# Depthwise convolution of a Conformer block: three of eight channel chunks moved from tap-by-tap accumulation to block Toeplitz products on TensorE over four token phases

## What is computed

```python
CONV_WIDTH = 31
def conv_module(x, w_pw1, b_pw1, w_dw, b_dw, ln_g, ln_b, w_pw2, b_pw2):
    h = x @ w_pw1 + b_pw1
    h = h[..., :D_MODEL] * jax.nn.sigmoid(h[..., D_MODEL:])
    h = lax.conv_general_dilated(
        h, w_dw[:, None, :], window_strides=(1,), padding=[(CONV_HALF, CONV_HALF)],
        dimension_numbers=('NWC', 'WIO', 'NWC'), feature_group_count=D_MODEL) + b_dw
    h = jax.nn.silu(layer_norm(h, ln_g, ln_b))
    return h @ w_pw2 + b_pw2
```

## Time and profile before

| | us |
|---|---|
| median of three runs | 2747.21 (2746.41 to 2748.06) |
| the profiled execution, first to last instruction | 2743.8 |
| convolution stage in it: from the first `up` of the second halves to the last `taps` | 563.0 to 746.0 |
| wait from there until `stats(0)` starts on PE | 4.6 |

### The profile page before, as it was taken

One profiled execution on the slowest core, in us unless ns is written; L12 is line 12 of the kernel. 1 busy time (PEld: TensorE's weight loads), 2 busy tenths in 40 slices (PEclk: granted clock), 3 DMA queues, 4 the chain that ended last, 5 costly groups with the idle time before them and its releaser, 6 DMA issues.

```text
span 2743.8 us, 36352 instructions
## 1 busy us (share of the span) xinstructions
PE 2665.3 (97%) x14266; PEld 2460.2 (90%) x14266; DVE 1423.0 (52%) x2553; ACT 986.2 (36%) x1647; POOL 1613.6 (59%) x874
## 2 busy tenths in 40 slices
PE   7999999999899999999999999999899999999998
PEld 7899999888678899999898999998899788999998
DVE  5643333669967643333664433337766476433335
ACT  4232332446543232332432322334445242323323
POOL 2576776669733576776636866674211234768665
PEclk9999999999999999999999999999999999999999
DMA  3222221311012222221421212232000111212213
GB/s 136 74 68 71 83 77 47 138 62 47 31 39 77 85 70 70 85 76 48 161 85 62 77 54 70 77 128 77 9 24 30 71 77 69 78 62 77 80 59 123
DMA packets 55464, 201.45 MB, mean 73 GB/s; under 512 B 6144, under 2 KB 6656, under 8 KB 55296
## 3 DMA queue, kind: packets, MB, share of 16 engines
q1 hardware_dynamic: 49248, 177.12, 19.5%
q10 hardware_dynamic: 6048, 22.02, 2.1%
HBM read 186.53 MB, written 12.58 MB: 73 GB/s over the span
## 4 chain that ended last, share of the span: by engine, by line
PE 80%; DVE 11%; POOL 5%; issue 3%; ACT 2%; DMA 0%; SPq 0%; POOLq 0%; DVEq 0%; ACTq 0%
PE ps L958 26%; PE ps L959 26%; PE ps L960 26%; POOL pacc L945 4%; DVE raw_sum L1625 2%; POOL w_lo L905 1%; DVE sum L1625 1%; DVE x L1643 1%; PE ps L1058 1%; DVE y L1632 1%; DVE y L1649 1%; PE ps L1194 1%; DVE pair L1523 0%; DVE xn L1696 0%; ACT w_hi L1252 0%
## 5 line engine op out<-in xcount | busy, mean ns | idle before, releaser
L905 POOL TENSOR_TENSOR w_lo<-w_stage,w_hi 128x1024 fp32r<-128x1024 f32 (+1 forms) x455 | 1019.3, 2268 | 576.1 <-ACT w_hi L1252 570.1
L958 PE MATMUL ps<-xn,w_hi 128*128 128x384 f32 x1920 | 646.9, 337 | 5.7 <-issue 4.2
L959 PE MATMUL ps<-xn,w_hi 128*128 128x384 f32 x1920 | 643.3, 335 | 0.0
L960 PE MATMUL ps<-xn,w_lo 128*128 128x384 f32 x1920 | 642.9, 335 | 0.0
L1252 ACT ACTIVATE w_hi<-w_stage 128x1024 fp32r<-128x1024 f32 (+1 forms) x455 | 436.5, 983 | 79.2 <-POOL w_stage L916 55.0
L958 PE MATMUL ps<-w_hi,hid 128*128 128x512 f32 x1056 | 412.7, 391 | 4.9 <-DVE y L1637 3.4
L960 PE MATMUL ps<-w_hi,hid 128*128 128x512 f32 x1056 | 411.4, 390 | 0.0
L959 PE MATMUL ps<-w_lo,hid 128*128 128x512 f32 x1056 | 411.3, 390 | 0.0
L958 PEld LDWEIGHTS ps<-xn,w_hi 128*128 128x128 f32 x1920 | 361.5, 188 | 9.5 <-issue 7.8
L959 PEld LDWEIGHTS ps<-xn,w_hi 128*128 128x128 f32 x1920 | 361.6, 188 | 1.7
L960 PEld LDWEIGHTS ps<-xn,w_lo 128*128 128x128 f32 x1920 | 361.3, 188 | 0.0
(11 more groups left out here) (196 smaller groups left out, 4034.1 us busy)
## 6 DMA issues: line engine op xcount, KB each, us to landing
w_stage<-weights SPq DMA_DIRECT2D x311, 512.0 KB, 3.6
x_kept<-x ACTq DMA_DIRECT2D x18, 512.0 KB, 2.6
x<-x_kept ACTq DMA_DIRECT2D x18, 512.0 KB, 7.0
g_pre<-rows SPq DMA_DIRECT2D x7, 512.0 KB, 5.3
x<-x_in SPq DMA_DIRECT2D x6, 512.0 KB, 7.9
g_post<-rows SPq DMA_DIRECT2D x6, 512.0 KB, 5.5
x<-x_in ACTq DMA_DIRECT2D x6, 512.0 KB, 8.0
y_out<-x SPq DMA_DIRECT2D x5, 512.0 KB, 2.6
```

The lines of the kernel that those rows point to most:

```text
L905: pool.tensor_tensor(w_lo[:, s, 0:n], w_stage[:, s, 0:n], w_hi[:, s, 0:n].bitcast(F32), ALU.subtract).then_inc(w_split, 1)
L958: pe.matmul(out, a[0], m[0], start=start, stop=False)
L959: pe.matmul(out, a[0], m[1], start=False, stop=False)
L960: return pe.matmul(out, a[1], m[0], start=False, stop=stop)
```

## The change

Chunks 0 to 4 lose their share on PE: all 31 taps go to DVE (20) and to ACT with POOL (11 products, 10 additions). Chunks 5 to 7 leave DVE, ACT and POOL altogether. For them `glu` writes the chunk in phase order (token 4n + i at phase i, place n); sixteen small DMAs a chunk on SP (`send`) regroup 32 channels x 4 phases onto the 128 partitions; for each of four groups of 32 channels DVE multiplies a 128x32 diagonal pattern with a table of tap values into nine 128x128 block Toeplitz matrices (`spread`, 1152 columns), PE makes nine products of 196 columns (`taps`), DVE takes the sums out with the bias (`gather`), and sixteen more small DMAs a chunk (`bring`, the last four on ACT's queue) carry them to `co`. `tap_w` and its building on ACT are gone. Input rows are put in phase order outside the kernel, and output rows back, so the order of tokens differs through the whole kernel; the work on them is the same outside the convolution. `stats` reads `co` with other addresses, 54 transposes in place of 48. The table `spread_in` is loaded before the stage's first weights, after a wait on the last pair product of the FFN ahead of it, and the rows `g_post` and `g_pre` are loaded at the end of the stage, since their places now hold the regrouped chunks.

```diff
-PE_TAPS = (0, 4, 4, 4, 5, 6, 8, 11)
-POOL_TAPS = (9, 9, 9, 9, 8, 8, 8, 10)
-DVE_TAPS = [TAPS - p - g for p, g in zip(PE_TAPS, POOL_TAPS)]
+CHAINS = 5
+POOL_TAPS = (11,) * CHAINS
+DVE_TAPS = [TAPS - g for g in POOL_TAPS]
...
+PHASES = 4
+GROUP = P // PHASES
+STEPS = 9
+SPREAD = STEPS * PHASES
...
         def taps(c):
-            s.add(1.34 * PE_TAPS[c], "taps", c)
-            tapped[c] = s.clock if c < KT - 1 else 0.0
-            splits()
...
+            for r in range(PHASES):
+                g = PHASES * (c - CHAINS) + r
+                s.add(3.05, "taps", c, r, g)
+                pool_until(s.clock)
+                dve_until(s.clock)
+                if g + 2 < GROUPS:
+                    on_dve(1.3, "spread", g + 2)
+                if r % 2 == 1:
+                    on_dve(0.6, "gather", c, r // 2)
+                splits()
...
         for c in range(2, KT):
             item(c, 0)
-            taps(c - 1)
-            if c > 2:
-                s.add(0, "tap_w", c)
+            if c == CHAINS + 1:
+                for g in range(2):
+                    on_dve(1.3, "spread", g)
+                taps(CHAINS)
             item(c, 1)
-        taps(KT - 1)
+        for c in range(CHAINS + 1, KT):
+            taps(c)
+        s.add(0, "bring_last")
...
+            def send(c):
+                to = phased[(c - CHAINS) % 2]
+                ...
+                sp.wait_ge(up_done, work.q[1, c, 1] + 1)
+                for r in range(PHASES):
+                    for j in range(PHASES):
+                        sp.dma_start(to[quarter(j), r, :], phases(c)[quarter(r), j, :]).then_inc(sent[c - CHAINS], 16)
+            def bring(c):
+                for a in range(2):
+                    sp.wait_ge(gathered, 2 * (c - CHAINS) + a + 1)
+                    for r in (2 * a, 2 * a + 1):
+                        ...
+                        for q in range(PHASES):
+                            sp.dma_start(out_place(c, r, q), sums_out(c)[quarter(q), r, :]).then_inc(brought[c - CHAINS], 16)
...
+                if u == UNIT0[1]:
+                    sp.wait_ge(pair_done, 4 * (CHUNKS - PLAIN) // 2)
+                    sp.dma_start(spread_v[:, :], spread_in).then_inc(spread_loaded, 16)
...
+                if u == row_unit(1, 3):
+                    send(CHAINS)
+                    bring(CHAINS)
+                elif u == row_unit(1, 5):
+                    send(CHAINS + 1)
+                elif u == row_unit(1, 7):
+                    send(CHAINS + 2)
+                    bring(CHAINS + 1)
+                    bring(CHAINS + 2)
+                    row(g_pre[:, :], PW2_ROW, pre_loaded)
+                    row(g_post[:, :], POST_ROW + 1, post_loaded)
...
+            def taps(c, r, g):
+                if r == 0:
+                    pe.wait_ge(sent[c - CHAINS], 16 * PHASES * PHASES)
+                if g >= PHASES and r % 2 == 0:
+                    pe.wait_ge(gathered, g // 2 - 1)
+                pe.wait_ge(spread_done, g + 1)
+                for m in range(STEPS):
+                    mm = pe.matmul(ps[:, 6 + r // 2, r % 2 * 2 * P:r % 2 * 2 * P + OUT_N],
+                                   spread_w[:, g % 2, m * P:(m + 1) * P],
+                                   phased[(c - CHAINS) % 2][:, r, m:m + OUT_N], start=m == 0, stop=m == STEPS - 1)
...
+            def spread(g):
+                if g >= 2:
+                    dve.wait_ge(taps_full, g - 1)
+                diagonal = spread_v[:, GROUPS * SPREAD:GROUPS * SPREAD + GROUP]
+                dve.tensor_tensor(spread_w[:, g % 2, :].rearrange("p (s n) -> p s n", s=SPREAD),
+                ...
+                                  ALU.mult).then_inc(spread_done, 1)
```

More of the change, by code:

```diff
@@ L374, in dve_until @@
             nonlocal dve
-            while dve < clock and at_d[0] < inputs[0] and at_d[0] in tapped:
+            while dve < clock and at_d[0] < inputs[0]:
                 c, j = at_d
-                if j == 0:
-                    dve = max(dve, tapped[c])
                 if j < DVE_TAPS[c]:
@@ L399, in item @@
             dve_until(s.clock + 0.7)
-            s.add(0, "glu", b, c, half, s.q[b, c, half])
-            dve += 0.7
+            while half == 0 and at_d[0] < c + 1 - CIN_SLOTS:
+                dve_until(dve + 1)
+            on_dve(0.9, "glu", b, c, half, s.q[b, c, half])
             if half == 1:
-                inputs[0] = c + 1
+                inputs[0] = min(c + 1, CHAINS)
             splits()
         def taps(c):
-            s.add(1.34 * PE_TAPS[c], "taps", c)
-            tapped[c] = s.clock if c < KT - 1 else 0.0
-            splits()
-        s.add(0, "tap_w", 1)
+            for r in range(PHASES):
[8 more added lines that the diff above has]
+                splits()
         item(0, 1)
-        s.add(0, "tap_w", 2)
         item(1, 1)
@@ L582, in plan, with trunk @@
     return s
-def trunk(nc, x_in, weights, vectors, rows, rope_in, ident_in, y_out, x_kept):
+def trunk(nc, x_in, weights, vectors, rows, rope_in, spread_in, ident_in, y_out, x_kept):
     work = plan()
@@ new lines, in glu, with gated @@
+                gated(c, q, ((near, 0, PHASES, NEAR), (far[:, 0:1, :], PROMPT, 1, P)) if half == 0
+                      else ((far[:, 1:, :], 0, PHASES - 1, P),))
+            def gated(c, q, parts):
+                for to, f, i, n in parts:
+                    a, gate = (t[:, f:f + i * n].rearrange("p (i n) -> p i n", i=i)
+                               for t in (ps[:, 2 * (q % 2), :], act_out[:, q % 2, :]))
+                    ins = dve.scalar_tensor_tensor(to, a, v("b_pw1", c), gate, ALU.add, ALU.mult)
+                ins.then_inc(up_done, 1)
@@ new lines, in glu_phased @@
+            def glu_phased(c, half, q):
+                if half == 0:
+                    dve.wait_ge(conv_done, c + 1 - CIN_SLOTS)
+                    for n in (0, FAR, IN_N - PHASES):
+                        dve.memset(phases(c)[:, :, n:n + PHASES], 0.0).then_inc(pads, 1)
+                near = phases(c)[:, :, PHASES:PHASES + NEAR]
+                far = phases(c)[:, :, FAR + PHASES:FAR + PHASES + P]
+                gated(c, q, ((near, 0, PHASES, NEAR), (far[:, 0:1, :], PROMPT, 1, P)) if half == 0
+                      else ((far[:, 1:, :], 0, PHASES - 1, P),))
@@ L1905, in _ @@
                     convolved(*at)
+                elif kind == "spread":
+                    spread(*at)
+                elif kind == "gather":
+                    gather(*at)
                 elif kind == "stats":
@@ L2007 @@
     column("w_dw", a["l0_conv_w_dw"].reshape(TAPS, KT, P).transpose(1, 0, 2))
+    w_dw, b_dw = a["l0_conv_w_dw"], a["l0_conv_b_dw"]
+    by_tap = np.zeros((PHASES, GROUP, GROUPS, SPREAD), np.float32)
+    bias = np.zeros((PHASES, GROUP, GROUPS), np.float32)
+    for g in range(GROUPS):
+        c0 = CHAINS * P + g * GROUP
+        for j in range(PHASES):
+            for n in range(SPREAD):
+                if 0 <= n + j - PHASES < TAPS:
+                    by_tap[j, :, g, n] = w_dw[n + j - PHASES, c0:c0 + GROUP]
+            bias[j, :, g] = b_dw[c0:c0 + GROUP]
+    diagonal = np.concatenate([np.eye(GROUP, dtype=np.float32)] * PHASES)
+    spread = np.concatenate([by_tap.reshape(P, -1), diagonal, bias.reshape(P, -1)], 1)
     rows = np.zeros((ROWS, D_MODEL), np.float32)
```

181 lines of the change are left out of this document (113 added, 68 removed).

## The result

The changed kernel took 2754.07 us (median of 12 runs, 2749.12 to 2758.02) against 2748.27 for the kernel before on the same chip (12 runs): 1.0019 times as long, with a 95% interval of 1.0011 to 1.0026. The forecast was 2746.6 and "no measurable change". The time lies inside the range (2734 to 2758), but what was measured is a loss of 3 to 7 us where a gain of 0.6 was forecast.

The account below looks back on a forecast made before the run. DVE's list with its late sigmoids was taken as the bound. From 2747.2 us, -2.5 in the stage, +0.65 at stats(0) and +1.2 at the stage's start gave 2746.6, range 2734 to 2758.

Parts of the forecast that it names:

- DVE as the bound, with its ledger: Convolution stage: DVE's work of 146.7 us plus 24.3 of waits puts the last sums out at 744.7; gain 2.5 us.
- The six waits: DVE's waits in the stage, for late sigmoids, a POOL addition and PE's use of the first matrices: together 24.3 us.
- PE's 20 us turned into waits: PE in the stage: 20.2 us less work, but it all becomes waits, about 13 us of them ahead of taps(5).
- Spread: Twelve spreads on DVE: 1.40 us each, 16.8 in all, plus 6.0 for the six that run beside POOL.
- Rival C: Spread and POOL shut each other out; a spread beside POOL takes 3.5 us: +10, 2756.6 us; chance 0.15.
- glu with a stride: glu on DVE, output stride of four elements: no extra time taken, at most 0.3 us each, 4 in all.
- An issue of a small DMA: SP's small DMAs for regrouping chunks: issues 0.47 us apart, the last landing 2.0 us later.
- rival D: An issue of the small DMAs takes 1 us rather than 0.47; taps(5) starts 8 us later: 2761 us; chance 0.07.
- stats(0) and behind: End of the stage: stats(0) starts 2.5 us earlier, then its three extra transposes cost 0.65 us.
- The start of the stage: Ahead of the stage: first weights land later, at about 509, making DVE's addition late: +1.2 us, bounds 0 and 5.

Follow-up runs that it names:

- e1: The changed kernel again, no edit, for a second profile: 2751.03 us, ratio 1.0011 to the kernel before.
- f1: e2 with the planner booking 2.25 us (even chunks) and 1.95 (odd) per POOL addition instead of 1.85: 2739.53 us, ratio 0.9961 to before.
- f2: e2 with 2.5 and 1.95 us booked per POOL addition, POOL's taps shared unevenly over chunks, each glu planned 1.7 us earlier: 2738.36 us, ratio 0.9959.
- f3: e2 with spread writing only 128 of 1152 columns from the third group on (output wrong, same matmuls): 2749.43 us, ratio 0.9999 to before.
- f4: e2 with PE doing up(6,1) ahead of taps(5) instead of behind it: 2752.45 us, ratio 1.0015 to before.
- e2: The changed kernel with SP's wait for the feed-forward pair and the table load eight weight units later: 2747.26 us, ratio 0.9999 to before.
- e3: The kernel before plus only SP's wait for the last feed-forward pair ahead of the stage's first weights: 2754.23 us, ratio 1.0021 to before.
- h1: f2 with ACT issuing rows 2 and 3 of send(7) and rows 0 and 2 of bring(7), SP the rest: 2738.79 us, ratio 0.9963.
- e4: The kernel before again, no edit, for a second profile: one run of 2746.08 us.
- g1: The kernel before with 2.25 us (even chunks) and 1.95 (odd) booked per POOL addition instead of 1.9: 2748.08 us, ratio 0.9996 to before.
- g2: f2 with ACT issuing rows 2 and 3 of send(7) and rows 0, 1 and 3 of bring(7), SP the rest: 2738.04 us, ratio 0.9964.
- g3: f2 once more, no further edit, for a second profile and more runs: 2738.43 us, ratio 0.9961 to the kernel before.

## Why the prediction was wrong

By its own steps:

- **DVE as the bound, with its ledger: right.** Forecast 174.4 us from `glu(1,1)` to the end of the last `convolved`; measured 755.30 - 580.63 = 174.7, and 174.8 in e1. The six waits were forecast at 10.0, 3.3, 1.2, 4.0, 3.4 and 2.4 (24.3) and came at 9.7, 2.9, 1.0, 2.9, 3.1 and 3.5 (23.2). f1 to f4 show that the mechanism is the one named. That the sum fits to 0.3 us is part luck: in that stretch DVE was busy for 147.1 us and not busy for 27.6, where 150.1 and 24.3 had been counted.
- **PE's 20 us turned into waits: right.** 13.4 us ahead of `taps(5)` (13 forecast). A group took 12.21 / 4 = 3.05 at the full clock (2.9 forecast from 0.160 a record; it is 0.170), the first four 14.1 with waits and half the clock (13.3).
- **Spread: right in sum.** The last six took 9.3 us, four of them 1.36 or less and two 1.9 and 2.0; the first six 14.6, that is 6.5 more than six times 1.35, against the 6.0 allowed. By the rule quoted from the Trainium skill, "SBUF — State Buffer", "Who interferes with whom", the trace agrees (1.36 alone, 2.62 to 2.88 at 682 to 694, where POOL is busy throughout). Rival C used the same rule, and its 10 us did not come.
- **glu with a stride: at its upper bound.** 0.93 us for 384 columns in chunks 0 to 4, where the output has a stride of four elements, 0.62 in chunks 5 to 7 and before. I took none and kept 0.3 each as a bound; it is 0.3, some 2 us over the seven in the ledger.
- **An issue of a small DMA: 0.63 us, not 0.47.** The sixteen of `send(5)` were issued from 674.6 to 684.1 and landed by 686.0. By the difference it moved `taps(5)` by 2.4 us, and f4 gives no sign that this cost anything; rival D, at 1 us an issue, did not come.
- **stats(0) and behind: right.** Up to `stats(0)` the stage gained 1.9 to 2.0 us against before (2.5 forecast), and up to `down` it gave back 0.9 to 1.2 (0.65 forecast).
- **The start of the stage: the step that failed.** Forecast +1.2, with bounds 0 and 5; measured 3.1 and 3.7 in the two profiles up to `glu(1,1)`, 3.3 to 3.8 in time by e2, and 5.8 to 7.4 by e3 in the kernel before. I followed the chain to the first row only: weights at 509, a split on ACT, two on POOL, the gain at 517.2, the addition. That part was nearly right (in e1 the weights landed at 509.5, the gain ended at 517.9 and the addition was 2.1 late). What I put at nothing is what POOL's late work does to DVE beside it: the next two splits stretched the addition by 0.9, and the gain of the second row, late by 5.2, held a small DVE instruction for 2.1. The wait for that gain is not the reason: by my own durations it would have ended at 522.0 + 2.4 = 524.4, and before, DVE used it only at 523.4, so it would have added nothing to the 1.2. I had priced this contention for `spread` (rival C), where it cost nothing in time, and not here, where DVE had no slack.
- **Not foreseen at all:** 4.7 to 4.8 us near 1975, in the three profiles of the changed kernel (the first, e1 and e2).

Sum, with e1: -1.9 + 0.9 + 3.1 + 4.8 = +6.9 in the profile (7.1 read, beside 0.3 of earlier shift), and +4.2 in time in e1, +5.8 in the first measurement. Without the failed step (e2) the change is within 0.1% of before in time, which is what its other terms said. How much of the loss near 1975 is in those times is not known.

## What to carry to other kernels

When a change puts a wait ahead of a load, follow the load through every engine that consumes it, and past the first thing that becomes late: here DVE waited 2.1 us for the first late row, and lost another 3.0 because POOL's late work now ran beside DVE instructions that it holds up. When work is taken from one of several engines that were matched, the planner's numbers have to be fitted again before the change is judged: one number (1.85 to 2.25 and 1.95) was worth 10 us after the change, 5 of them seen in the queues, and nothing that could be measured before it. A long wait on the engine that was relieved can be a symptom of who feeds it: here moving its work (f4) only changed which engine was named as the cause.

## What was not expected of the hardware

**The clock near 1975.** The two longest idle times of PE are the same in both kernels there. Timeline rows of PE's transposes of the attention, in the changed kernel and then in before, and the granted clock in stretches (columns as above) of the changed kernel and of before:

```profile
1952.49 0.73 PE L1240 MATMUL ps<-ident,act_out 128*128 128x128 f32 x4 [2.12 <-DVE act_out L1960]
...
1971.40 0.66 PE L1240 MATMUL ps<-ident,act_out 128*128 128x128 f32 x4 [2.96 <-DVE act_out L1960]
```
```profile
1946.29 0.66 PE L1139 MATMUL ps<-ident,act_out 128*128 128x128 f32 x4 [2.12 <-DVE act_out L1822]
...
1965.21 0.66 PE L1139 MATMUL ps<-ident,act_out 128*128 128x128 f32 x4 [2.97 <-DVE act_out L1822]
```
```profile
1952.90:1956.30 3.40, 3.40 (x11) 2.73 (x10) 3.32 (x7) 1.24 (x3) 3.02 (x5) 0.50 0.00 0
1976.80:1987.10 10.30, 10.30 (x46) 10.30 (x45) 1.74 (x5) 3.32 (x6) 0.00 (x0) 0.50 0.00 0
```
```profile
1965.70:1969.10 3.40, 3.40 (x13) 3.40 (x12) 2.67 (x7) 1.73 (x4) 0.00 (x0) 0.50 0.00 0
```

After the same idle times, 2.12 and 2.96 us, the clock fell to 1.2 GHz for 3.4 us at the second in before, and in the changed kernel at the first, and then for 10.2 us some 5 us behind the second, although PE had been idle only 1.3 us in between. (Before had a third idle time, 1.5 us at 1957.5, which the changed kernel, slower there, did not have.) The long stretch stands in the profiles of the changed kernel, e1, e2 and h1, and in none of before, e3, e4, f1 to f4, g1, g2 and g3, where one stretch of 3.4 us stands instead. It costs 4.7 to 4.8 us. Whether the program sets it or chance does, and how many of the timed runs had it, stays open: nothing here could switch it. The timed runs show that a kernel moves by as much by itself: the ten of g1 fall into five of 2744.9 to 2746.0 and five of 2750.2 to 2751.2, and beside e1 seven of the 25 runs of before took 2752.2 to 2754.5 (the median is 2746.8), three of them at a mean granted clock of 0.990 to 0.991, which is that of the changed kernel (0.989 to 0.992), where the 15 fastest had 0.994 to 0.996. So a difference of 5 us between two single profiles is no proof of a difference between two kernels.

**A stride of 16 bytes** on the output made a DVE instruction of 384 float32 columns 0.93 us long instead of 0.62. The Trainium skill, "SBUF — State Buffer", "Door 1: The DMA port swizzle", says that accesses which cross to a new line of 16 bytes each time pay a penalty; the trace agrees.

**Sixteen small DMAs** of 32 rows go out 0.63 us apart and take 1.8 us to land, so the regrouping of a chunk (0.4 MB) takes some 12 us between two engines. Sharing them between SP and ACT made the last wait 1.4 us shorter (h1). By the Trainium skill, "DMA: Bandwidth & Descriptors", "Issuing engines are not separate DMA queues", issuing on several engines saves only the time of the issue, which is usually small beside the transfer; here the time of the issue was the larger part.
